# Two transformer blocks in float32: one more tile of each feed-forward stage by half-size products, with sums made earlier and in another place

## The reference, cut to what matters

```python
def swiglu(h, w_gate, w_up, w_down):
    return (jax.nn.silu(h @ w_gate) * (h @ w_up)) @ w_down

x = x + 0.5 * swiglu(rms_norm(x, ffn1_norm[l]), ffn1_w_gate[l], ffn1_w_up[l], ffn1_w_down[l])
# ... mixer (w_in, convolutions, sparse attention, w_out), cross attention (wq, wkv, wo) ...
x = x + 0.5 * swiglu(rms_norm(x, ffn2_norm[l]), ffn2_w_gate[l], ffn2_w_up[l], ffn2_w_down[l])
# second block: mixer (w_in_2, retention, differential attention, w_out_2), then
h = h + (jax.nn.silu(u @ w_gate[l]) * (u @ w_up[l])) @ w_down[l]
```

## Time and profile before

| | |
|---|---|
| median of 3 runs | 3421.53 us (3419.54 to 3421.73) |
| the profiled execution | 3419.55 us, span 3417.6 us |
| PE busy | 3363.7 us, 98% of the span |
| DVE busy | 2478.2 us, 73% |
| ACT busy | 1682.3 us, 49% |
| POOL busy | 783.1 us, 23% |
| 16 DMA engines, mean share of queue 1 and 0 | 32.8%, 17.2% |

### The profile page before, as it was taken

One profiled execution on the slowest core, in us unless ns is written; L12 is line 12 of the kernel. 1 busy time (PEld: TensorE's weight loads), 2 busy tenths in 40 slices (PEclk: granted clock), 3 DMA queues, 4 the chain that ended last, 5 costly groups with the idle time before them and its releaser, 6 DMA issues.

```text
span 3417.6 us, 53591 instructions
## 1 busy us (share of the span) xinstructions
PE 3363.7 (98%) x20506; PEld 2917.1 (85%) x20506; DVE 2478.2 (73%) x3862; ACT 1682.3 (49%) x2647; POOL 783.1 (23%) x651
## 2 busy tenths in 40 slices
PE   9999999999999999999999999999999999999998
PEld 7899786879899989978687989977899898889987
DVE  5678887558678967889756866865587685567865
ACT  4455366346445644536534644534464453455544
POOL 0011394112012301239412201220220031031103
PEclk9999999999999999999999999999999999999999
DMA  5376432336676667633242666622275672237654
GB/s 161 98 180 148 110 105 62 111 87 142 148 169 159 150 145 172 158 102 99 68 117 81 147 151 164 154 74 69 74 164 146 146 170 83 62 83 182 148 144 115
DMA packets 657033, 431.54 MB, mean 126 GB/s; under 512 B 17456, under 2 KB 620488, under 8 KB 656840
## 3 DMA queue, kind: packets, MB, share of 16 engines
q1 hardware_dynamic: 617096, 317.08, 32.8%
q0 software_dynamic: 35712, 106.45, 17.2%
q10 hardware_dynamic: 4032, 5.51, 0.7%
HBM read 314.68 MB, written 2.10 MB: 93 GB/s over the span
## 4 chain that ended last, share of the span: by engine, by line
PE 84%; DVE 6%; issue 5%; POOL 3%; ACT 1%; DMA 0%; POOLq 0%; SPq 0%; ACTq 0%; DVEq 0%
PE bank L585 14%; PE bank L587 14%; PE bank L586 14%; PE bank L626 11%; PE bank L628 11%; PE bank L627 11%; POOL mem L2428 1%; PE bank L753 1%; PE bank L755 1%; PE bank L754 1%; DVE u_lo L1628 1%; POOL mem L2353 1%; POOL mem L2352 1%; PE bank L738 1%; DVE x L1765 1%
## 5 line engine op out<-in xcount | busy, mean ns | idle before, releaser
L1166 ACT ACTIVATE w_hi<-raw 128x1024 fp32r<-128x1024 f32 (+1 forms) x403 | 375.9, 933 | 543.6 <-PE bank L587 524.9
L587 PE MATMUL bank<-h_hi,w_lo 128*128 128x512 f32 (+1 forms) x1568 | 608.3, 388 | 0.0
L585 PE MATMUL bank<-h_hi,w_hi 128*128 128x512 f32 (+1 forms) x1568 | 606.9, 387 | 0.7 <-DVE w_lo L1624 0.7
L586 PE MATMUL bank<-h_lo,w_hi 128*128 128x512 f32 (+1 forms) x1568 | 602.8, 384 | 0.0
L2386 POOL DMA_DIRECT2D w_lo<-raw x248 | 216.0, 871 | 1620.1 <-ACT w_lo L1174 1619.9
L585 PE MATMUL bank<-u_hi,w_hi 128*128 128x512 f32 x1008 | 405.7, 403 | 8.2 <-DVE u_lo L1628 6.6
L1137 ACT ACTIVATE w_hi<-raw 128x1024 fp32r<-128x1024 f32 x199 | 209.0, 1058 | 415.9 <-PE bank L587 409.4
L587 PE MATMUL bank<-u_hi,w_lo 128*128 128x512 f32 x1008 | 401.0, 398 | 0.0
L586 PE MATMUL bank<-u_lo,w_hi 128*128 128x512 f32 x1008 | 398.7, 396 | 0.0
L626 PE MATMUL bank<-t_hi,sum_hi 128*128 128x256 f32 x1368 | 379.8, 278 | 0.6 <-DVE sum_lo L1711 0.6
L627 PE MATMUL bank<-t_lo,sum_hi 128*128 128x256 f32 x1368 | 379.5, 277 | 0.0
(11 more groups left out here) (297 smaller groups left out, 7898.4 us busy)
## 6 DMA issues: line engine op xcount, KB each, us to landing
w_lo<-raw POOLq DMA_DIRECT2D x158, 512.0 KB, 6.4
raw<-in_w_in SPq DMA_DIRECT2D x96, 512.0 KB, 3.8
raw<-in_ffn_w_gate SPq DMA_DIRECT2D x88, 512.0 KB, 4.0
raw<-in_ffn_w_up SPq DMA_DIRECT2D x88, 512.0 KB, 5.2
raw<-in_ffn_w_down SPq DMA_DIRECT2D x64, 512.0 KB, 5.4
w_lo<-raw POOLq DMA_DIRECT2D x90, 256.0 KB, 4.1
raw<-in_w_gate SPq DMA_DIRECT2D x44, 512.0 KB, 3.9
raw<-in_w_up SPq DMA_DIRECT2D x44, 512.0 KB, 5.1
```

The costliest lines, as they stand in the source:

```text
L585: mm(o, w_hi[:, s, w], rhs_hi[:, r], start=k == order[0], stop=False)
L586: mm(o, w_hi[:, s, w], rhs_lo[:, r], start=False, stop=False)
L587: ins = mm(o, w_lo[:, s, w], rhs_hi[:, r], start=False, stop=k == order[-1])
L1166: ins = a(w_hi[:, to % RING, part], raw[:, to % RING, part], ACT.Copy)
```

## The change

1. `fast_tiles` begins at tile 1 in group 0: one more tile, in five stages, by half-size products.
2. The activation sums are made in `t_source`, a part of `mem` that the rests `t_lo` then overwrite in place; `sums` is no longer written. ACT no longer waits for the rests of T before it rounds weight sums.
3. The weight sums of tile 1 are made at the end of what stands before the stage: DVE makes them behind `u_lo(6)`, ACT rounds them behind its last tile.
4. DVE's order at the stage's start: the four T sums first, then `norm_scale`, then the rests.
5. PE waits for each rest of T by itself. In the first stage's first down chunks the rounding and the rests of T come one to two chunks later (ACT at k = 4 to 7, DVE two each at k = 6 and 7).
6. At the ends of the feed-forward stages ACT squares `x(k)` into two buffers, and POOL only adds (`sum_squares`).
7. Down chunks of a last group (6 row blocks) are rounded only over 768 of 1024 columns (`SHORT`).

The diff, cut to its core:

```diff
-    return range(0 if g else 2, F_GROUPS[g][1]) if q or g else range(0)
+    return range(0 if g else 1, F_GROUPS[g][1]) if q or g else range(0)
...
+T_USED = (T1, T2, T3, T4)
...
-    return slice(HC if up else 0, CH)
+    return slice(HC if up else 0, F_GROUPS[-1][1] * P if c in SHORT else CH)
...
+        squared = y_buf
...
-        u_half = sums.rearrange("p (k s n) -> p k s n", s=2, n=HS)
+        t_source = view(6656, KT * S)
+        u_half = t_source.rearrange("p (k s n) -> p k s n", s=2, n=HS)
...
+        t_lo = [t_lows[:, 0:4, 0, :], t_lows[:, 0:4, 1, :], t_lows[:, 4:8, 1, :], t_lows[:, 4:8, 0, :]]
... fast_pair (PE)
-                pe.wait_ge(t_split, T_COUNT * (FAST[q] + 1))
+                t0 = T_COUNT * FAST[q]
+                pe.wait_ge(t_split, t0 + 1)
                 pe.wait_ge(s_split, m * 2 + 1)
                 product(m5, summed_w(S1), summed_u(T1)).then_inc(w_mm, 1)
+                pe.wait_ge(t_split, t0 + 2)
...
                 product(m6, summed_w(S2), summed_u(T2)).then_inc(w_mm, 1)
                 pe.wait_ge(s_split, m * 2 + 2)
                 product(m3, summed_w(S4), plain_u(1, 1)).then_inc(w_mm, 1)
+                pe.wait_ge(t_split, t0 + 3)
...
+                pe.wait_ge(t_split, t0 + 4)
... ffn (ACT), group 0
+                        if fast:
+                            for i in range(T_COUNT):
+                                round_summed(q, i)
                         next_weights(n + 1)
...
-                        if fast:
-                            act.wait_ge(t_split, T_COUNT * (FAST[q] + 1))
-                            for half in range(2):
-                                sums_rounded(PAIR[n + RING], half)
... ffn (ACT), end of the stage
                             finish(q + 1, k, gain + k)
+                            if k >= 2:
+                                act.wait_ge(sq_sum, 8 * q + k - 1)
+                            a(squared[k % 2], tile(x, k), ACT.Square).then_inc(tile_squared, 1)
                             source(q + 1, k, gain + k)
-                        if not (q or g) and k in (3, 4, 5, 6):
-                            round_summed(q, T_ORDER[k - 3])
+                        if not (q or g) and k >= 4:
+                            round_summed(q, k - 4)
...
+                    if q + 1 in FAST and end:
+                        first_sums_rounded(n + 8 + 2)
... ffn (DVE), group 0
-                        next_low(n)
-                        if q:
-                            norm_scale(q)
-                        if fast:
-                            for j in T_ORDER:
-                                summed(q, j)
+                    if fast and g == 0:
+                        first = PAIR[n + 2]
+                        for j in T_ORDER:
+                            summed(q, j)
+                        norm_scale(q)
+                        rest_of_sums(first, 0)
+                        for i in range(2):
+                            rest_of_summed(q, i)
                         v.wait_ge(rstd_set, q + 1)
                         gate(n, 0)
+                        rest_of_summed(q, 2)
                         up(n + 1, 0)
+                        rest_of_summed(q, 3)
+                        rest_of_sums(first, 1)
                         rest_of_tile(0, 0)
+                        weight_sums(n + RING)
... ffn (DVE), down chunks
-                            if k in (3, 4, 5, 6):
-                                rest_of_summed(q, T_ORDER[k - 3])
                             if k in (2, 3, 4, 5):
                                 summed(q, T_ORDER[k - 2])
+                            elif k >= 6:
+                                for i in range(2 * k - 12, 2 * k - 10):
+                                    rest_of_summed(q, i)
                         if end:
                             finish(q + 1, k, gain + k)
+                            if k == 6 and q + 1 in FAST:
+                                weight_sums(n + 8 + 2)
... plain_finish (DVE)
                     finish(q, k, gain + k)
+                    if k == 6 and q in FAST:
+                        weight_sums(n + 8 + 2)
... sum_squares (POOL)
+                for k in range(KT):
+                    if q == 8:
+                        pool.wait_ge(j_squared, k + 1)
+                        chain.done(pool, tt(j_sum, j_sum, tile(j_sq, k), ALU.add))
+                    pool.wait_ge(tile_squared, SQUARED[q] + k + 1)
+                    if k:
+                        pool.wait_ge(sq_sum, 8 * (q - 1) + k)
+                    tt(sumsq, sumsq, squared[k % 2], ALU.add).then_inc(sq_sum, 1)
```

More of the change, by code:

```diff
@@ L174, in ffn_tables @@
                 low += range(c + RING, c + 2 * fn + RING)
-            c = c + 2 * fn + 8
-    return pairs, low
-PAIR, LOW = ffn_tables()
+            c = c + 2 * fn
+            if fn < KT:
+                short += range(c, c + 8)
+            c = c + 8
+    return pairs, low, short
+PAIR, LOW, SHORT = ffn_tables()
+SQUARED = {q + 1: 8 * i for i, q in enumerate(FFN_AT)}
 def part_of(c):
     up = c in PAIR and PAIR.get(c - 1) == PAIR[c]
-    return slice(HC if up else 0, CH)
+    return slice(HC if up else 0, F_GROUPS[-1][1] * P if c in SHORT else CH)
 def low_count(c):
@@ L1158, in source @@
                 if q in FAST:
-                    a(tile(sums, k), tile(x, k), ACT.Copy, scale=col(gain)).then_inc(t_src, 1)
+                    a(tile(t_source, k), tile(x, k), ACT.Copy, scale=col(gain)).then_inc(t_src, 1)
             def high(c):
@@ L1178, in next_weights, with sums_rounded, first_sums_rounded @@
                 negated(c)
+            def sums_rounded(m, half):
+                act.wait_ge(s4_made if half else s_made, m + 1)
+                if m:
+                    act.wait_ge(w_mm, m * 5 - 2 + 2 * half)
+                at = slice(half * CH, half * CH + CH)
+                a(sum_hi[:, at], w_sum[:, at], ACT.Copy).then_inc(s_rounded, 1)
+            def first_sums_rounded(c):
+                for half in range(2):
+                    sums_rounded(PAIR[c], half)
             def ffn(n, q, f, gain, more=True, joint=False):
@@ L1256, in ffn @@
                         for k in range(KT):
-                            a(tile(sums, k), tile(x, k), ACT.Copy, scale=col(G_FFN1 + k)).then_inc(t_src, 1)
+                            a(tile(t_source, k), tile(x, k), ACT.Copy, scale=col(G_FFN1 + k)).then_inc(t_src, 1)
                     for k in range(KT):
@@ L2363, in squares @@
                     chain.done(pool, nc.gpsimd.memset(j_sum, 0.0))
-                with chain.loop(pool, 0, 2, 8 if q == 8 else 4) as i:
+                for k in range(KT):
[6 more added lines that the diff above has]
+                    tt(sumsq, sumsq, squared[k % 2], ALU.add).then_inc(sq_sum, 1)
+                pool.wait_ge(sq_sum, 8 * q)
+            def squares(n, q):
+                pool.wait_ge(taken, n + RING + 1)
+                clear_sum()
+                with chain.loop(pool, 0, 2, 4) as i:
                     for j in range(4):
-                        if q == 8:
-                            pool.wait_ge(j_squared, i * 4 + (j + 1))
-                            chain.done(pool, tt(j_sum, j_sum, tile(j_sq, i * 4 + j), ALU.add))
                         pool.wait_ge(taken, At(n + j, i).no + RING + 1)
@@ L2393, in fast_parts @@
                         if g == 0:
-                            for c in range(n, n + RING):
+                            for c in range(n, n + 2):
                                 low_part(c + RING)
```

112 lines of the change are left out of this document (44 added, 68 removed).

## The result

The changed kernel takes 3431.66 us (median of 6 runs, 3429.11 to 3434.67) against 3420.53 for the kernel before (3412.03 to 3421.73), a ratio of 1.0034 with a 95% interval of 1.0024 to 1.0045: 11 us slower, some 3 us more than the 3428.7 of the sum. Its profiled execution took 3431.31 us.

A forecast was written before the change was run, and what follows sets the result against it. The prediction took PE, busy 98%, as the bound, held up by waits for other engines at stage starts and ends. It summed -6.9 + 13.3 + 8.6 + 2.2 - 10 = +7.2 us on 3421.5: 3428.7, range 3415 to 3440.

The forecast's parts named there:

- PE's own work: One more tile by half-size products in five stages, a pair taking 9.82 us against 11.20: 6.9 us less.
- DVE at a stage's start: Five stage starts: PE waits 0.5 us at the spread and 2.0 before m3; with next pair's m5, 13.3 us more.
- the first T sum: Stage starts: four T sums summed at 4.78 us; some 0.5 us slower start beside late POOL named, not summed.
- the reason given for m3: Stage starts: DVE's eight instructions ahead of the needed weight-sum rest take 8.1 us against PE's 6.1, a 2.0 us wait.
- The weight sums: Before five stages: four additions behind u_lo(6) delay the last u_lo, 0.75, 0.9, 0.75, 3.1 and 3.1, 8.6 us in all.
- The first stage: First pair: two rests of T at k = 7 delay the rest of the weight sums, 2.2 us more.
- The fourth stage's end: Squares on ACT relieve POOL and DVE; PE's two waits shrink to about 1 us: 10 us gained, bounds 3 and 11.
- Rival C, the clock: Waits of about 3 us at first, fifth and sixth stages drop PE's clock: three falls, +6, 3435; chance 0.13.
- A: Stage starts: the gain stands but DVE finishes ahead of PE: 3404.6, or 3417 with half the waits; chance 0.14.
- B: Fourth stage's end: little relief, PE still waits 7 to 8 of the 11.2 us, 3436; chance 0.13.
- D: Whole kernel: no measurable change, waits at lower bounds and relief at its upper, +0.6, 3422; chance 0.15.

The follow-up runs named there:

- rest_early: Changed kernel with the second rest of the first weight sums made before the first gate instead of after the last activation rest; 3432.2 us, 1.0038.
- rest_early_less: rest_early with two of the four additions of the second pair's first weight sums left out in five stages (a price test); 3427.2 us, 1.0024.
- sums_late: Changed kernel with the first weight sums' four additions made after the last u_lo of the stage before instead of ahead of it; 3436.6 us, 1.0049.
- sums_split: Changed kernel with the first weight sums' additions spread: one after k = 4, one after 5, two after 6; 3431.9 us, 1.0036.
- first_rests: Changed kernel with the first stage's four activation rests and their rounding moved back to the fifth, sixth and seventh tile; 3428.7 us, 1.0024.
- The squares alone: Kernel before with one part of the change: ScalarE squares the tiles at the feed-forward stages' ends, GpSimd only adds; 3406.4 us, 0.9962.
- before_all_squares: Kernel before with ScalarE's squares at every stage end and nothing else of the change; 3408.2 us, 0.9964.
- squares_back: Changed kernel with the squares undone: GpSimd squares and adds at every stage end again; 3440.7 us, 1.0061.
- plain_squares: Changed kernel with ScalarE's squares used at the other five stage ends too; 3423.0 us, 1.0008.
- combo4: Changed kernel with five DVE moves: first stage's rests early, weight sums spread, two activation sums earlier, second weight rest before the first gate; 3429.5 us, 1.0027.

## Why the prediction was right, and where its steps were not

The waits, their places and the gain at the fourth stage's end came as forecast, so the mechanism holds in the main. That the number came within 3 us is partly luck. Over the seven stretches the sum was 8.2 us short; 3.8 us of "all else", which no step had forecast and which differs between kernels that are equal there, took back nearly half of it. And at the fourth stage's end the profiled execution escaped a fall of the clock worth 1.6 us that six other kernels with the same code and the same wait there had.

**PE's own work, -6.9.** Right as a row: a pair still takes 9.82 us. But no kernel ran with this part alone, so its worth in time is argued from the rows, not measured by itself.

**DVE at a stage's start, +13.3.** The waits stand where they were forecast: m3 starts 1.8 us late in three stages (2.0 forecast), 0.9 in two, where PE itself came later. At the spread PE starts 1.4 us late in the second and fourth stage, not 0.5. From U on each start is 2.4 to 3.0 us longer, where 2.7 - 1.4 = 1.3 was forecast: that is most of what my sum lacked, 6.9 us of 8.2 over the seven stretches. The mis-sized term is the first T sum, 2.31 us (1.85 in the third stage, 2.31 in the other four) in place of 1.2, which is about 5 of the 6.9 us; the half clock of the fifth and sixth stage, 0.7 us each, is most of the rest. DVE's chain from U to the last rest of sums takes 17.15 us in the second stage, where 16.3 was summed. The prediction named this term in its paragraph on the fourth stage's end, at some 0.5 us, and left it out of the sum; no run takes POOL's last add away from beside the T sum, so its price is read from the rows:

```profile
788.74 1.22 DVE L1637 TENSOR_TENSOR w_lo<-raw,w_hi 128x1024 fp32r<-128x1024 f32 x1
789.87 1.53 DVE L1641 SCALAR_TENSOR_TENSOR u_lo<-x,par,u_hi 128x512 fp32r<-128x512 f32 x1
791.33 2.31 DVE L1732 TENSOR_TENSOR mem<-mem 128x1024 f32<-128x1024 f32 x1
793.67 1.22 DVE L1735 TENSOR_TENSOR mem<-mem 128x1024 f32<-128x1024 f32 x1
```

What failed beside it is the reason given for m3: that the order of eight instructions ahead of it sets the wait. rest_early takes that reason away and gains nothing; rest_early_less gains what leaves DVE's sum. Had I carried DVE's list on to the second pair I would have seen that it has no pause but the 1.13 us up to a rest that, in the changed kernel, ends 0.05 us before PE needs it, so that no order of this list could have helped.

**The weight sums, +8.6.** To U they cost 0.3, 0.8, 0.3, 3.3 and 3.3 us, 7.9 in all, where 0.75, 0.9, 0.75, 3.1 and 3.1 were forecast. The step holds, with DVE's pauses taking up more than I gave them. Of the two other places tried, sums_late is worse over the five stages together, and sums_split is better only where DVE has pauses (1.2 us in the second and fourth stage) and worse in the other three.

**The first stage, +2.2.** The wait grew from 0.57 to 2.84 us, 2.3 as forecast; the half clock behind it is the other 1.3. first_rests gives all of it back.

**The fourth stage's end, -10.** -9.2, with the one wait of 1.97 us in place of "about 1" and the clock at 1.00. Nine other kernels have this code and this wait (1.95 to 1.99 us). In six of them the clock fell there, and the stretch is -7.5 or -7.6; where it did not, it is -9.0 to -9.2. So the place gives 7.5 to 9.2, by the clock. The squares alone give 8.3 without a fall and, in before_all_squares, 6.6 with one. Like with like that leaves 0.9 us for the narrower rests (0.95 us in the first of the two rows above) and what else is changed. squares_back has one fall there, as six of the others have: the squares are worth 7.5 - 1.9 = 5.6 us then, and 7.3 against the changed kernel, which had none.

**Rival C, the clock.** The falls came, behind 2.84 and twice 2.94 us of waiting as that rival had it, and one more in the third stage; the time did not. At half clock the 128x512 matmuls start 0.43 us apart in place of 0.23, which loses 1.4 us of the 3.0 from 1141.80 and 2.9 of the 6.5 from 2490. But from U on the third stage is only 0.1 us longer than the second, the fifth and sixth 0.7: while PE is slow DVE catches up, and the waits at the spread and before m3 shrink by what the clock takes. The same code shows it: in first_rests and plain_squares the clock did not fall in the third stage, and from U on it takes 80.75 us as in the changed kernel, where it did; in rest_early it fell in the fifth and sixth, and they take no longer than the second (80.65 and 80.66 against 80.64). Where no wait for DVE follows, the price is whole: 1.3 us in the first stage, 1.6 in the fourth of rest_early and at the fourth stage's end. Of +6 some 2.7 came. What that rival lacked is the question what the slower engine owes next.

**Rivals A, B and D** are out: A by the waits, B by the one wait of 1.97, D by an interval that does not hold a ratio of 1.

## What to carry to other kernels

When a second engine works without a pause from one stage into the next, follow its list until its first pause and compare whole sums; single waits on the way are where the sum shows, not what it costs, and a new order moves them. Of a change with several parts, measure the part that relieves the bound by itself: here it was worth 11 to 14 us without its companions (6.6 to 8.3 of them at the one place that it was made for), which took 20 and more. GpSimd work beside a full VectorE list is to be priced as VectorE's own. A fall of PE's clock costs little while PE would be waiting anyway.

## What the runs showed of the hardware

**GpSimd and VectorE take turns, whole instruction by whole instruction.** POOL in the stretch of the DVE rows just above:

```profile
789.09 1.76 POOL L2366 TENSOR_TENSOR mem<-x 128x512 f32 x1 [4.07 <-DVE x L1752]
790.93 1.62 POOL L2367 TENSOR_TENSOR mem<-mem 128x512 f32<-128x512 f32 x1
```

w_lo ended at 789.96; POOL's square, issued at 789.09, ended 0.89 us after that (790.85). u_lo, issued at 789.87, ended 0.55 after the square (791.40). POOL's add, issued at 790.93, ended 1.15 after u_lo (792.55). The T sum, issued at 791.33, ended 1.09 after the add (793.64). So each printed duration holds a wait for the end of the other engine's instruction: the T sum's 2.31 us are 1.22 of waiting and 1.09 of work. The same arithmetic gives the additions at 1.78 in sums_split (POOL's add ended at 2473.57 and the addition at 2474.12, 0.55 later), and in plain_squares POOL's 1.86 (u_lo ended at 2476.11, plus 1.15 is 2477.26) and the 1.79 behind it (plus 0.55 is 2477.81). It also gives DVE's 3.69 us per tile ahead of the fifth stage (0.89 + 0.55 + 1.15, and 1.09 for the rest of the chunk, one instruction behind the other), and why four additions in a row are cheaper than four single ones: only the first meets an instruction of POOL. All these DVE instructions read two tensors in SBUF. The residual, which reads one of its two from `bank` in PSUM, takes 0.68 us also beside POOL (at 2475.25 in the kernel before, while POOL's add ran from 2474.86 to 2476.48).
The Trainium skill has the rule behind this (SBUF — State Buffer, Who interferes with whom): the port pair that the two engines share is an exclusive lock, issue order decides who blocks, and a VectorE instruction with two inputs in SBUF contends with a GpSimd instruction that reads SBUF. That whoever issues first has the pair for the whole instruction it says of VectorE's two-port modes; the rows here show it for two inputs in SBUF. The trace agrees: the own times read from four steps of one kernel give the ends of two instructions of another to 0.01 us. The prediction had read another page of the Trainium skill (GPSIMD Engine Reference, Key points), which speaks of contention only, and made 0.5 us of it, where the T sum then waited 1.2.

**The same wait is followed by a fall of the clock in one kernel and not in the next.** At the fourth stage's end of first_rests, PE's wait and the window behind it, then the window behind the wait of 1.97 us in the changed kernel, where the code and the wait are the same:

```profile
2244.75 0.80 PE L594 MATMUL bank<-u_hi,w_hi 128*128 128x512 f32 x1 [1.98 <-DVE u_lo L1642]
2244.80:2248.00 3.20, 3.20 (x8) 2.52 (x9) 0.42 (x1) 1.06 (x1) 2.56 (x2) 0.50 0.56 164
```

```profile
2251.20:2258.00 6.80, 6.80 (x31) 5.57 (x32) 1.70 (x1) 1.26 (x2) 2.58 (x2) 1.00 0.52 150
```

It fell after 0.92 + 0.17 us of waiting in the third stage of the changed kernel and not after the same waits there in first_rests, plain_squares and rest_early; it fell after one of 1.93 us in combo4, and not after 1.23 and 1.67 in the second stage of the changed kernel. So the length of a wait alone doesn't tell, and one fall more or less (1.6 us at this place) is not to be read as an effect of an edit. What decides is left open here.
